# 62 instead of 26 of the 128 half operations on gathered rows in the scoring stage, on one Trainium2 core

## The chip, the cores and the metric

The kernel runs on one core of one Trainium2 chip. The metric is the device time of one execution in microseconds, the median of several runs. The engines are TensorE (PE; PEld is its weight load), VectorE (DVE), ScalarE (ACT), GpSimd (POOL) and SyncE (SP), which here only issues loads.

## What is computed

One residual block on 256 tokens of width 2048: a mixing layer (attention and a gated part), then a PEER retrieval layer with 16384 experts, then a final norm. The change is in the retrieval layer:

```python
def one_block(xb):
    q = (xb @ w_q).reshape(T, PEER_HEADS, 2, PEER_HALF)
    sc = jnp.einsum('thcd,hckd->thck', q, sub_keys)
    ...
    idx = e1 * PEER_N_KEYS + e2
    g = jax.nn.softmax(best.astype(jnp.float32), axis=-1)
    u_sel = jnp.take(u_tab, idx, axis=0)
    act = jax.nn.gelu(jnp.einsum('td,thkd->thk', xb, u_sel))
    v_sel = jnp.take(v_tab, idx, axis=0)
    return jnp.einsum('thk,thkd->td', g.astype(act.dtype) * act, v_sel)
```

Each token picks 8 x 16 = 128 experts. A row of `peer_u` per pick gives a score, and the rows of `peer_v`, weighted by gate times gelu of the score, are summed.

## The kernel before

Two groups of tokens are treated in two ways. For ND = 224 tokens nothing is gathered: the kernel multiplies with all 16384 rows of both tables and lets the gates be zero where a row was not picked. For the other NS = 32 tokens the picked rows are gathered: 32 tokens x 4 slots fill the 128 partitions, and NG = 32 rounds bring one row of `peer_u` and later one of `peer_v` to each partition. Every row comes in two halves of 1024 numbers, so there are 4 x NG = 128 half operations: numbers 0 to 63 on `peer_u` (a product with the token and a sum, L1079), and 64 to 127 on `peer_v` (scaled and added to an accumulator, L1082 and L1085). `half_rows(k)` on VectorE does number k; `gather(k)` on GpSimd (L386) brings its 0.52 MB (128 rows of 4 KB) into one of the two halves of the tile PICKED, as soon as half operation k-2 has read it.

**Scoring stage** (about 470 to 1244 us). 128 steps j, each with two units of `u_t`, 0.52 MB each, through a ring of six slots. SP loads a unit (L321) when the slot's former unit is used up; ACT rounds it to its high part (HI, `top`, L588); VectorE subtracts for the low part (RING_LO, `low`, L1032); TensorE does eight high matmuls (L1428) and, one unit later, eight low ones (L1434). When both units of step j are through, ACT copies the low half of the result (`low_half_out`, L622, tile HOLES), VectorE adds it (`sum_halves`, L1042), ACT applies gelu. Behind the sum stand, at steps from 2 on, pieces of the choice of experts, and, at the steps named in HALF_STEPS, one half operation.

From step SPREAD0 = 60 to 115 the gates of the 224 tokens are also spread over the 16384 experts, four tokens a step: VectorE multiplies the product of the step before into the store (`apply_gates`, L1060) and makes second one-hots (L1050); ACT puts the rest of that product (`put_gates`, L647, which waits for L1060) and makes first one-hots (L632, L635); TensorE multiplies the two (`spread`, L1398, into a PSUM bank); VectorE also gates the newest scores (`land`, L1068). Each engine runs its queue in the order of the code. In ACT's loop a step is:

```python
            for j in range(NKEYS):
                top(2 * j + 4)
                if j:
                    gelu(j - 1)
                if 0 <= j - 1 - SPREAD0 < N_BATCH:
                    put_gates(j - 1 - SPREAD0)
                if 0 <= j - SPREAD0 < N_BATCH:
                    first_one_hots(j - SPREAD0)
                top(2 * j + 5)
                low_half_out(j)
```

and in VectorE's: the two `low` of step j+1, `apply_gates`, `second_one_hots`, `land`, `sum_halves(j)`, the half operation.

**Value stage** (about 1244 to 1957 us). 256 units v of `peer_v` (a half of the columns for each of the 128 steps, then the other half) go through the same ring and the same `top` and `low`. Here the stored products are the moving operand: ACT rounds them (`weight_hi`, L681, tile WHL), VectorE makes their remainder (`weight_lo`, L1116), TensorE does eight high matmuls (L1468) and, one unit later, eight low ones (L1473). In ACT's queue `weight_hi(v+3)` stands behind `top(v+4)`, so TensorE's unit v+3 waits for the load of unit v+4. The half operations that are not in the scoring stage stand at the units in HALF_UNITS, spread evenly. Between the two halves of columns VectorE empties eight banks (L1122).

GpSimd's queue holds, in order: some `low` (until step 60), the first gathers, the two loads of X1R behind the end of the scoring stage, the other gathers, with the load of FG among them.

Of the kernel before, what the change touches and what calls it, by code (L numbers as in the profile page):

```python
# [26 lines left out]
PH, TOPK, NKEYS = 8, 16, 128  # L27
# [43 lines left out]
SPREAD0 = 60  # L71
SPREAD_END = SPREAD0 + N_BATCH
# [16 lines left out]


HALVES = 4 * NG
HALF_STEPS = list(range(SPREAD0 + 2, SPREAD_END, 4)) + list(range(SPREAD_END, NKEYS))
HALF_UNITS = [1 + i * 248 // (HALVES - len(HALF_STEPS)) for i in range(HALVES - len(HALF_STEPS))]
LAST_DOT = HALF_UNITS[2 * NG - 1 - len(HALF_STEPS)]
S_BANKS = 3
# [21 lines left out]
def hybrid_peer_block(nc, x, w_in, w_out, wq_t, keys_t, u_t, peer_u, peer_v, ws_t, bs_t, gain_t, ffn_gain, z_gain,  # L117
                      out_gain, subln_gain, final_gain, lambdas, rope, out):
    ctx = ExitStack()
    with ctx:  # L120
# [210 lines left out]
        def _(pool):  # L331
# [48 lines left out]
            def gather(k):  # L380

                table = peer_u if k < 2 * NG else peer_v
                g, half = k % (2 * NG) // 2, k % 2
                if k >= 2:
                    pool.wait_ge(halves, k - 1)
                pool.indirect_dma_start(PICKED[:, half * HALF:(half + 1) * HALF], None,  # L386
                                        table.rearrange("e (a c) -> (e a) c", a=2),
                                        bass.IndirectOffsetOnAxis(PK4[:, half, g:g + 1], 0)).then_inc(row_ready[half], 16)
# [14 lines left out]
            pool.wait_ge(x4_scaled, 1)  # L403
            for k in range(len(HALF_STEPS) + 2):
                gather(k)
            pool.wait_ge(low_used, N_U)
            for tt in range(TT):
                pool.dma_start(X1R[:, tt, :], x1_dram[tt * P:(tt + 1) * P, :]).then_inc(x1_back, 16)
            for k in range(len(HALF_STEPS) + 2, HALVES):
                u = HALF_UNITS[k - 2 - len(HALF_STEPS)]  # L410
                if u >= NKEYS + 32 and HALF_UNITS[k - 3 - len(HALF_STEPS)] < NKEYS + 32:
                    pool.wait_ge(low_used, N_U + NKEYS + 24)
# [1142 lines left out]
```

## Time and profile before

| | |
|---|---|
| median of 3 runs | 1994.64 us (1987.77 to 2002.11) |
| profiled execution | 1981.4 us, span of its core 1979.6 us |
| PE / PEld busy | 93% / 85% |
| DVE, ACT, POOL busy | 69%, 53%, 18% |
| read from HBM | 421.29 MB, 215 GB/s over the span |
| gathers | 64 from peer_u, 64 from peer_v |

The profile shows one execution. Busy times count instructions at work; an idle time is put down to what ended it, as the semaphores tell. A matmul's time overlaps that of the next. PEclk is the clock that TensorE was granted, as a share of 2.4 GHz.

### The profile page before, as it was taken

How to read it: one execution, taken by the hardware profiler on the slowest of the kernel's cores; microseconds unless marked ns; L12 is line 12 of the kernel's file. 1: busy time of each engine (PE TensorE's matmuls, PEld its weight loads, DVE VectorE, ACT ScalarE, POOL GpSimd, SP SyncE). 2: the span in 40 equal slices, each digit the busy share in tenths (PEclk: the TensorE clock that was granted, in tenths of full speed). 3: DMA queues.
4: the chain of work that ended last, by engine and by line, in shares of the span. 5: the costliest groups of instructions: out<-in, count | busy, mean ns of one | idle time of the engine just before them, and what ended most of it. 6: DMA issues, size and time to landing. Idle time of an engine off the chain costs nothing. (4 is left out here: it accounts for less than half of the span.)

```text
span 1979.6 us, 29432 instructions
## 1 busy us (share of the span) xinstructions
PE 1846.3 (93%) x10926; PEld 1675.0 (85%) x10926; DVE 1368.1 (69%) x2269; ACT 1042.2 (53%) x1815; POOL 362.3 (18%) x213
## 2 busy tenths in 40 slices
PE   7999989899999999988898889899999999999996
PEld 6887777789989999888888889888988988888886
DVE  4446775654798888666666677776766777677676
ACT  5454644434555555766666664454444444444444
POOL 1003330100420530000000003222222222222220
PEclk9999999999999999999999999999999999999999
DMA  7665435765667676555555558887888878878883
GB/s 247 185 186 155 148 117 177 245 192 179 193 200 209 205 221 208 186 174 173 170 166 175 171 173 297 296 265 264 282 261 265 273 249 272 274 261 274 271 264 116
DMA packets 116197, 427.62 MB, mean 216 GB/s; under 512 B 13088, under 2 KB 13184, under 8 KB 115008
## 3 DMA queue, kind: packets, MB, share of 16 engines
q1 hardware_dynamic: 95472, 347.65, 55.7%
q0 software_dynamic: 20448, 77.67, 11.6%
q8 instruction: 84, 1.38, 0.3%
q10 hardware_dynamic: 144, 0.52, 0.1%
q14 instruction: 49, 0.40, 0.1%
HBM read 421.29 MB, written 4.51 MB: 215 GB/s over the span
## 5 line engine op out<-in xcount | busy, mean ns | idle before, releaser
L588 ACT ACTIVATE HI<-RING_RAW 128x1024 fp32r<-128x1024 f32 x512 | 541.9, 1058 | 544.6 <-DMA RING_RAW<-peer_v 372.3
L1032 DVE TENSOR_TENSOR RING_LO<-RING_RAW,HI 128x1024 fp32r<-128x1024 f32 x481 | 586.7, 1237 | 1.8
L1468 PE MATMUL PS<-WHL,HI 128*128 128x448 f32 x2048 | 472.8, 374 | 50.0 <-DVE WHL L1116 48.4
L1428 PE MATMUL PS<-xT,HI 128*128 128x448 f32 x2048 | 465.7, 369 | 0.0
L1468 PEld LDWEIGHTS PS<-WHL,HI 128*128 128x128 f32 x2048 | 371.2, 191 | 86.1 <-ACT HI L588 38.1
L1428 PEld LDWEIGHTS PS<-xT,HI 128*128 128x128 f32 x2048 | 366.4, 189 | 24.6
L1434 PEld LDWEIGHTS PS<-xT,RING_LO 128*128 128x128 f32 x2048 | 265.9, 191 | 16.2 <-DVE RING_LO L1032 4.4
L1473 PEld LDWEIGHTS PS<-WHL,RING_LO 128*128 128x128 f32 x2048 | 270.2, 192 | 7.2
L1434 PE MATMUL PS<-xT,RING_LO 128*128 128x224 f32 x2048 | 269.5, 274 | 2.6 <-DVE RING_LO L1032 1.8
L1473 PE MATMUL PS<-WHL,RING_LO 128*128 128x224 f32 x2048 | 271.0, 275 | 0.0
L735 DVE TENSOR_TENSOR LO<-RAW,HI 128x1024 fp32r<-128x1024 f32 x124 | 155.8, 1259 | 139.2 <-PE PS L1221 103.1
L421 ACT ACTIVATE HI<-RAW 128x1024 fp32r<-128x1024 f32 x144 | 153.1, 1065 | 168.1 <-PE PS L1221 56.4
L1116 DVE TENSOR_TENSOR WHL<-store,WHL 128x224 fp32r<-128x224 f32 x256 | 99.8, 390 | 204.2 <-ACT WHL L681 202.8
L386 POOL DMA_INDIRECT PICKED<-peer_u,PK x64 | 106.5, 1664 | 656.3 <-DVE DOTS L1079 655.9
L386 POOL DMA_INDIRECT PICKED<-peer_v,PK x64 | 110.0, 1720 | 324.2 <-DVE ACC L1085 305.9
L1216 PE MATMUL PS<-HI,xT 128*128 128x512 f32 x444 | 141.9, 401 | 1.7 <-ACT HI L421 1.0
L1221 PE MATMUL PS<-HI,xT 128*128 128x512 f32 x444 | 138.6, 394 | 0.0
L1042 DVE TENSOR_TENSOR TMP<-PS,HOLES 128x224 f32<-128x224 f32 x68 | 26.6, 392 | 140.7 <-ACT HOLES L622 139.9
L377 POOL TENSOR_TENSOR RING_LO<-RING_RAW,HI 128x1024 fp32r<-128x1024 f32 x31 | 74.6, 2407 | 251.5 <-DVE store L1042 251.5
L1398 PE MATMUL PS<-HOLES,ONE 128*128 128x128 f32 x448 | 64.6, 287 | 38.8 <-ACT ONE L635 38.8
L1221 PEld LDWEIGHTS PS<-HI,xT 128*128 128x128 f32 x444 | 84.2, 190 | 18.2
L1216 PEld LDWEIGHTS PS<-HI,xT 128*128 128x128 f32 x444 | 81.2, 190 | 17.9 <-DVE xT L762 1.1
(204 smaller groups left out, 1683.6 us busy)
## 6 DMA issues: line engine op xcount, KB each, us to landing
RING_RAW<-u_t SPq DMA_DIRECT2D x256, 512.0 KB, 4.4
RING_RAW<-peer_v SPq DMA_DIRECT2D x256, 512.0 KB, 5.7
RAW<-w_in SPq DMA_DIRECT2D x80, 512.0 KB, 3.6
RAW<-w_out SPq DMA_DIRECT2D x32, 512.0 KB, 4.4
RAW<-wq_t SPq DMA_DIRECT2D x32, 512.0 KB, 4.4
x_spill<-X POOLq DMA_DIRECT2D x2, 1024.0 KB, 6.0
X1R<-x_spill POOLq DMA_DIRECT2D x2, 1024.0 KB, 7.2
out<-X1R SPq DMA_DIRECT2D x4, 512.0 KB, 3.7
```

The lines of the kernel that those rows point to most:

```text
L386: pool.indirect_dma_start(PICKED[:, half * HALF:(half + 1) * HALF], None, table.rearrange("e (a c) -> (e a) c", a=2), bass.IndirectOffsetO ...
L421: nc.scalar.activation(HI[:, slot, :], RAW[:, slot, :], ACT.Copy).then_inc(hi_ready, 1)
L588: nc.scalar.activation(HI[:, n % HI_SLOTS, :], RING_RAW[:, n % RING, :], ACT.Copy).then_inc(top_ready, 1)
L735: v.tensor_tensor(LO[:, u % 2, :], RAW[:, u % 4, :], HI[:, u % 4, :].bitcast(FP32), ALU.subtract).then_inc(lo_ready[u % 2], 1)
L1032: v.tensor_tensor(RING_LO[:, n % RING, :], RING_RAW[:, n % RING, :], HI[:, n % HI_SLOTS, :].bitcast(FP32), ALU.subtract).then_inc(low_dve, 1)
L1116: v.tensor_tensor(WHL[:, u % W_SLOTS, 1, :], store[:, u % NKEYS, :], WHL[:, u % W_SLOTS, 0, :].bitcast(FP32), ALU.subtract).then_inc(w_lo, 1)
L1216: mm(banks[c], high(tt), h[:, halves[c]], start=first, stop=False)
L1221: ins = mm(banks[c], low(tt), h[:, halves[c]], start=False, stop=last and tt > 0)
L1428: return mm(PS[:, j % S_BANKS, 0:2 * ND].rearrange("p (a t) -> p a t", a=2), HI[:, n % HI_SLOTS, kk * P:(kk + 1) * P], xT[:, k, :, 0:ND], ...
L1434: return mm(PS[:, j % S_BANKS, 0:ND], RING_LO[:, n % RING, kk * P:(kk + 1) * P], xT[:, k, 0, 0:ND], start=False, stop=k == KT - 1)
L1468: return mm(PS[:, V_BANKS[i], 0:2 * ND].rearrange("p (a t) -> p a t", a=2), HI[:, v % HI_SLOTS, i * P:(i + 1) * P], WHL[:, v % W_SLOTS, :, :],
L1473: return mm(PS[:, V_BANKS[i], 0:ND], RING_LO[:, (N_U + v) % RING, i * P:(i + 1) * P], WHL[:, v % W_SLOTS, 0, :], start=False, stop=v % NKE ...
```

## The change

```diff
 HALVES = 4 * NG
-HALF_STEPS = list(range(SPREAD0 + 2, SPREAD_END, 4)) + list(range(SPREAD_END, NKEYS))
+HALF_STEPS = list(range(SPREAD0 + 6, NKEYS))
 HALF_UNITS = [1 + i * 248 // (HALVES - len(HALF_STEPS)) for i in range(HALVES - len(HALF_STEPS))]
```

SPREAD0 is 60, SPREAD_END 116, NKEYS 128. HALF_STEPS was 62, 66, ... 114 (14 steps) and 116 to 127 (12); it is now 66 to 127 (62). HALF_UNITS follows: 102 units 2 or 3 apart before, 66 units 3 or 4 apart now. Everything else that depends on the number (the split of GpSimd's queue, the unit at which the dots are finished: 90 before, 4 now) is computed from it.

VectorE's queue at the first of the changed steps, step 62: L1042 is the sum of step 62, L1079 the half operation with its read of the sum (two rows), L1032 the subtractions for step 63.

```order
 L1068 TENSOR_TENSOR store<-store,TMP 128x8
 L1042 TENSOR_TENSOR TMP<-PS,HOLES 128x224
-L1079 ISA PICKED,DOTS<-PICKED,X_96 128x1024
-L1079 ISA DOTS 128x1
 L1032 TENSOR_TENSOR RING_LO<-RING_RAW,HI 128x1024 x2
 L1060 TENSOR_TENSOR store<-store,PS 128x62x4
```

The half operation of step 62 is gone. The same queue at step 67 and the start of step 68:

```order
 L1068 TENSOR_TENSOR store<-store,TMP 128x28
 L1042 TENSOR_TENSOR TMP<-PS,HOLES 128x224
+L1079 ISA PICKED,DOTS<-PICKED,X_96 128x1024
+L1079 ISA DOTS 128x1
 L1032 TENSOR_TENSOR RING_LO<-RING_RAW,HI 128x1024 x2
 L1060 TENSOR_TENSOR store<-store,PS 128x67x4
```

Between the sum and the subtractions for the next step there is now a half operation, and so it is at every step to 115 that had none.

GpSimd's queue from the return of the picks (PK) on; x_spill is where X1R is loaded from:

```order
 L400 DMA PK_107<-spk_spill 32x3x32 x4
 L377 TENSOR_TENSOR RING_LO<-RING_RAW,HI 128x1024 x9
-L386 DMA PICKED<-peer_u,PK_107 128x1024 x28
+L386 DMA PICKED<-peer_u,PK_107 128x1024 x64
 L408 DMA X1R<-x_spill 128x2048 x2
-L386 DMA PICKED<-peer_u,PK_107 128x1024 x36
-L386 DMA PICKED<-peer_v,PK_107 128x1024 x30
+L386 DMA PICKED<-peer_v,PK_107 128x1024 x43
 L413 DMA FG<-final_gain 128x2048
```

The loads of X1R stand behind all 64 gathers of peer_u now, and only gathers of peer_v are left behind them.

## Rows read from the trace of the kernel before

**Rows 1.** Busy us by stage: window, length, PE, PEld, DVE, ACT, POOL, PEclk, DMA share, GB/s.

```profile
800.00:1181.00 381.00, 342.19 (x2219) 318.53 (x2218) 252.56 (x524) 259.46 (x607) 23.48 (x14) 1.00 0.56 174
1181.00:1244.00 63.00, 56.71 (x360) 53.28 (x358) 51.02 (x77) 32.60 (x53) 18.82 (x12) 0.99 0.83 283
1244.00:1952.00 708.00, 663.70 (x4055) 620.85 (x4056) 503.75 (x659) 336.44 (x507) 173.21 (x104) 0.99 0.80 266
```

**Rows 2.** Timeline, a step without half operation: start us, us, engine, line, operation [idle before].

```profile
1110.62 0.34 ACT L622 ACTIVATE HOLES<-PS 128x224 f32<-128x224 f32 x1
...
1111.04 0.39 DVE L1042 TENSOR_TENSOR TMP<-PS,HOLES 128x224 f32<-128x224 f32 x1 [2.21 <-ACT HOLES L622]
1111.35 2.35 DVE L1032 TENSOR_TENSOR RING_LO<-RING_RAW,HI 128x1024 fp32r<-128x1024 f32 x2
...
1113.62 0.58 DVE L1060 TENSOR_TENSOR store<-store,PS 128x420 f32<-128x420 f32 x1
...
1116.31 1.04 ACT L588 ACTIVATE HI<-RING_RAW 128x1024 fp32r<-128x1024 f32 x1
1116.46 1.16 PE L1398 MATMUL PS<-HOLES,ONE 128*128 128x128 f32 x8 [0.45 <-ACT ONE L635]
1117.26 0.34 ACT L622 ACTIVATE HOLES<-PS 128x224 f32<-128x224 f32 x1
```

**Rows 3.** Timeline of the value stage around one late load.

```profile
1634.28 7.87 SPq L321 DMA_DIRECT2D RING_RAW<-peer_v  x4
...
1636.60 1.79 PE L1468 MATMUL PS<-WHL,HI 128*128 128x448 f32 x8
...
1639.11 1.79 PE L1468 MATMUL PS<-WHL,HI 128*128 128x448 f32 x8
...
1641.61 1.06 ACT L588 ACTIVATE HI<-RING_RAW 128x1024 fp32r<-128x1024 f32 x1 [3.51 <-DMA RING_RAW<-peer_v]
...
1642.98 0.39 DVE L1116 TENSOR_TENSOR WHL<-store,WHL 128x224 fp32r<-128x224 f32 x1 [3.32 <-ACT WHL L681]
...
1643.52 1.66 PE L1468 MATMUL PS<-WHL,HI 128*128 128x448 f32 x7 [1.73 <-DVE WHL L1116]
```

**Rows 4.** Line L1468: count, min/median/max ns, first and last start us.

```profile
L1468 PE MATMUL PS<-WHL,HI x2048: 358/365/742, 1244.1 to 1956.1; 128*128 128x448 f32 x187
```

**Rows 5.** Loads by median us to landing, in 500 to 700, 1250 to 1934, 1935 to 1955.

```profile
RING_RAW<-u_t SPq DMA_DIRECT2D x76, 512.0 KB, 4.5
...
RING_RAW<-peer_v SPq DMA_DIRECT2D x246, 512.0 KB, 5.7
...
RING_RAW<-peer_v SPq DMA_DIRECT2D x4, 512.0 KB, 4.9
```

**Rows 6.** Timeline, a step with a half operation.

```profile
1173.17 0.39 DVE L1042 TENSOR_TENSOR TMP<-PS,HOLES 128x224 f32<-128x224 f32 x1 [2.14 <-ACT HOLES L622]
1173.48 1.22 DVE L1079 CUSTOM_DVE_ANT_0 PICKED<-PICKED,X 128x1024 f32<-128x1024 f32 x1
...
1179.74 1.16 PE L1398 MATMUL PS<-HOLES,ONE 128*128 128x128 f32 x8 [1.59 <-ACT ONE L635]
...
1180.96 0.39 DVE L1042 TENSOR_TENSOR TMP<-PS,HOLES 128x224 f32<-128x224 f32 x1 [2.12 <-ACT HOLES L622]
```

**Rows 7.** The sum of step 60; then groups of 800 to 1181: busy, mean ns, idle before.

```profile
800.11 0.39 DVE L1042 TENSOR_TENSOR TMP<-PS,HOLES 128x224 f32<-128x224 f32 x1 [2.22 <-ACT HOLES L622]
...
L1398 PE MATMUL PS<-HOLES,ONE 128*128 128x128 f32 x448 | 64.6, 287 | 38.8 <-ACT ONE L635 38.8
...
L1079 DVE CUSTOM_DVE_ANT_0 PICKED<-PICKED,X 128x1024 f32<-128x1024 f32 x14 | 17.0, 1216 | 0.0
```

**Rows 8.** Timeline: TensorE's first matmuls of the value stage.

```profile
1244.12 6.15 PE L1468 MATMUL PS<-WHL,HI 128*128 128x448 f32 x16 [5.82 <-DVE WHL L1116]
```

**Rows 9.** GpSimd's timeline: two of the gathers that begin late behind the former.

```profile
1259.95 1.71 POOL L386 DMA_INDIRECT PICKED<-peer_u,PK  x1 [7.52 <-DVE DOTS L1079]
...
1884.09 1.68 POOL L386 DMA_INDIRECT PICKED<-peer_v,PK  x1 [7.82 <-DVE ACC L1085]
```

## The prediction

> **What bounds the kernel now.** I read, in this order, a table of busy time by stage, the timeline of single steps, the groups of instructions with the idle time before them, and the times that loads take to land. The reader should see in the table that TensorE (PE) is the busiest engine, and where it is not full: 342.2 of 381.0 us while the gates are spread (800 to 1181), 663.7 of 708 in the value stage [rows 1]. These two stretches have different limits, and the change takes work from the second and puts it into the first.
>
> In the spreading stretch the timeline of one step without a half operation shows a ring that goes through two engines [rows 2]. From one low-half copy on ScalarE (ACT, L622) to the next the starts are: sum on VectorE (DVE, L1042) 0.42 us later, its two subtractions (L1032) 0.31 later, the gating product (L1060) 2.27 later; then on ACT, behind that product, the put (L647), the first one-hots (L632, L635) and the next rounding (L588), which starts 2.69 later, and the next copy 0.95 after it. That is 6.64 us, the whole step, with no slack: each item waits for the one before it, or stands behind it in its queue. TensorE is not in the ring. It waits 0.45 us in each such step for the one-hots, before its eight spreading products (L1398). VectorE is idle too, 2.2 us in each step, but ahead of the sum, where it waits for the copy.
>
> In the value stage TensorE sets the pace when nothing is late: a unit (eight high and eight low matmuls) starts 2.51 us after the one before, 1636.60 to 1639.11 [rows 3]. All 2048 high matmuls start between 1244.1 and 1956.1, 712.0 us [rows 4]; 255 units at 2.51 and the last unit's 1.4 make 641.5. So 70.5 us are lost. The releasers of the idle time are DVE's WHL and ACT's HI, and both stand behind a DMA. The rows of one loss show it: a load of peer_v issued at 1634.28 lands, and ACT rounds it at 1641.61, 7.33 us later; only behind this rounding, in ACT's queue, comes the weight (L681) of the unit before, then DVE's remainder of it (L1116) at 1642.98, and TensorE starts at 1643.52 instead of 1641.62, 1.90 us late [rows 3]. So a load has 7.33 less 1.90, about 5.4 us, to land. The median load of this stage takes 5.7, in the last 20 us, where no gather is left, 4.9, and the u_t loads of a stretch without gathers took 4.5 [rows 5]. The gathers are what pushes loads over the limit.
>
> **What moves.** From the code: before, 14 half operations stand at steps 62, 66 to 114 and 12 at steps 116 to 127; now one stands at each step 66 to 127, which keeps the last 12 and has 50 in place of 14 in the spreading stretch, 36 more. The value stage has 66 instead of 102. Nothing is added in all, and each gather on GpSimd's queue moves with its half operation, two ahead.
>
> **The scoring stage.** The moved operation (L1079) stands right behind the sum, inside the ring: sum at 1173.17, half operation at 1173.48 [rows 6], and the subtractions only behind that. The step from sum to sum is 1180.96 less 1173.17, 7.79 us, against 6.64 without one [rows 2, 6]. TensorE waits 1.59 instead of 0.45. The long row agrees: from the sum of step 60 (800.11) to that of step 115 (1180.96) are 55 steps, 380.85 us [rows 6, 7]; 55 at 6.64 are 365.2, and 15.7 us for the 14 half operations [rows 7] are 1.12 each. I take 1.14, from the added wait of TensorE. VectorE's 2.2 us of idle time do not cover it: that wait ends with ACT's copy, which moves too. 36 times 1.14 is **+41.0 us**. The bounds are narrow, 39 to 43: the 36th, at step 115, leads into a step that lacks the one-hots and may be half hidden, and longer waits could come from the gathers. The latter I cost at nothing: a gather is issued two half operations ahead, 15.5 us now, and lands in under 10; the DMA moved 174 GB/s in this stretch [rows 1], and 3 transfers of 0.52 MB in 7.8 us are 202 GB/s, which the stretch without gathers also moved (76 loads of 0.52 MB in 200 us) [rows 5].
>
> Steps 116 to 127 keep 12 half operations in both kernels, and TensorE was busy 56.7 of 63 us there, 5.8 of the rest being one wait at the changeover [rows 1, 8]: 0, give or take 2. On GpSimd's queue the two X1R loads now stand behind 64 gathers instead of 28, but the last of them is released at step 127 in both; 0. The change of the dots into gates comes at units 4 and 8 instead of 90 and beyond, with the same instructions; 0 to 1.
>
> **The value stage.** It loses 36 half operations and 36 gathers. VectorE is busy 503.8 of 708 us there [rows 1] and not the bound, so its 36 times 1.3 us are worth nothing by themselves; what is regained is the late loads. Of the 70.5 us lost about 2 are the first units at half clock [rows 8] and about 4 the flush between the two halves of columns; 64.5 remain for the 101 gathers issued in this stage, 0.64 us each. Their neighbours stand 2 or 3 units apart. If the price is per gather, 36 fewer give back 36 times 0.64, **-23.0 us**. Both ends are open, since the trace has no gather that stands alone: a gather may cost as much as the one loss shown, 1.9 us for the two gathers in flight, that is 0.95 each, so that 65 of them cost 62 and only 3 us come back; or half of today's price when its neighbour is far off, 21 in all, so that 44 come back. I take 0.64, as it is the mean of all of them: by the timeline the 14 gathers that stand more than 9 us behind the one before (first and last in [rows 9]) were followed by 0.68 us of loss each, the other 84 by 0.66.
>
> **Sum.** 41.0 less 23.0 is +18.0 us. The profiled execution took 1981.4 us for its span of 1979.6, so 1999.4. It is faster than all three timed runs, whose median is 1994.6, 13.2 above; the sum goes onto the median: 2012.6, and I say 2012, +0.9%.
>
> **Rivals.** (a) *The losses stay.* The loads go on being late, one stall for each gather that stands alone, where now two gathers 4 us apart share one. At 0.95 each the stage gives back 3 us and the kernel is +38 us, 2033. It decides from 0.66 us a gather on: there 64.5 less 65 times 0.66 is 21, the net 20, and the kernel over 1% slower. For it speaks the shown stall, and that 5.4 us is only 0.5 above the unloaded 4.9; against it that many gathers pass without any stall. The Trainium skill has a rule that would lead to the same end, on the page "DMA: Bandwidth & Descriptors", section "Latency and other measured facts": reads from HBM whose rows lie a large power of two apart ran at 207 GB/s for a 512 KiB pitch and 164 for 2 MiB. A load of peer_v has a pitch of 1 MiB, and by that rule the loads alone would need 2.5 to 3.2 us a unit, gathers or not; the time would come out near +41. The trace does not bear it out: the stage moves 266 GB/s, gathers included [rows 1], and units follow at 2.51 us wherever no load is late.
> (b) *Gathers that stand alone cost half.* Then 44 us come back, the net is -3, 1992, no change. For it speaks that a lone gather overlaps fewer loads; against it the 14 above.
> (c) *The half operation hides in VectorE's idle time*, or nearly no losses are left in the value stage. Either makes the net about -20: 1975, faster. Against the first stand the 14 steps of 7.8 us [rows 6]; for the second there is nothing but the distance.
> (d) *TensorE's clock falls.* It will wait 1.6 us in every one of 50 steps in a row instead of in every fourth. The granted clock was 0.5, that is 1.2 GHz, at the start of the value stage behind a wait of 5.82 us, and 16 high matmuls took 6.15 us there [rows 8], where eight take 1.79 [rows 3]. A step at this level is 6.15 for its 16 high matmuls, half of that for the 16 low ones with half the columns, and 1.2 for the spreading: 10.4, or 2.6 over the new step. In half of the 50 steps that is 65 us more, 2077. Against it: the 14 steps with 1.6 us of waiting had clock 1.00 throughout [rows 1]. The Trainium skill speaks against the change here ("TensorE: Matmul & The Clock Gate", section "A second HAM failure mode: psum-queue depth-cycling"): many short idle times between groups of matmuls made the clock swing. The row of today has none of it at one long wait in four; steps in a row are not shown.
>
> **How the numbers follow.** Forecast 0.64, with an own range of 2000 to 2024; (a) 0.16; (b) 0.12; (c) 0.04; (d) 0.04. A measurement of this kernel tells about 1%, 20 us, from no change. The forecast lies just inside; with its width some 0.24 of its 0.64 falls beyond. So slower 0.24 + 0.16 + 0.04 = 0.44, within 1% 0.40 + 0.12 = 0.52, faster 0.04. The range, 1991 to 2035, takes in (a) and (b) at their own values.
>
> **What would show it.** In the changed profile: sums (L1042) of steps 66 to 115 all 7.8 us apart, the idle time of L1398 from 38.8 us [rows 7] to near 38.8 + 36 times 1.14, 80 us; ACT and DVE rows in the same order as in [rows 6]; the value stage beginning 41 us later, near 1285, and lasting 689 us instead of 712. If the first holds and the value stage lasts over 700, (a) was right; under 675, (b) or (c). Clock 0.5 in rows of the spreading stretch would be (d). Steps of 6.7 us with half operations would overthrow the ring itself.

## The result, and the profile after

| | before | changed |
|---|---|---|
| runs | 1987.77, 2002.11, 1994.64, 1997.3 | 2014.72, 2027.51, 2024.31, 2033.8 |
| median us | 1995.97 | 2025.91 |
| profiled execution | 1981.4, span 1979.6 | 2014.7, span 2012.9 |

The ratio is 1.0148 with an interval of 1.0087 to 1.021: slower by 1.5%, 30 us. In the pair of profiled executions it is 33.3 us; the profiled one of the kernel before, 1981.4, is faster than all four of its timed runs, which matters below for what a single profile can tell. The forecast was +18.

The stages of the changed kernel, in the columns of [rows 1]; its scoring stage ends at 1282, not 1244. The rows are the spreading stretch and the value stage:

```profile
800.00:1222.00 422.00, 343.45 (x2222) 319.68 (x2221) 294.16 (x597) 258.58 (x606) 83.30 (x50) 1.00 0.60 200
...
1282.00:1988.00 706.00, 665.66 (x4077) 622.47 (x4077) 462.64 (x587) 337.35 (x508) 111.65 (x68) 0.99 0.75 240
```

In the value stage VectorE does 41 us less, GpSimd 62 us less, and the DMA moves 240 GB/s instead of 266. The stage is hardly shorter for it in this pair.

The spreading steps, first the sums of steps 60 and 115, then one step with its half operation, to be laid beside [rows 6]:

```profile
798.51 0.39 DVE L1042 TENSOR_TENSOR TMP<-PS,HOLES 128x224 f32<-128x224 f32 x1 [2.21 <-ACT HOLES L622]
...
1101.01 1.16 PE L1398 MATMUL PS<-HOLES,ONE 128*128 128x128 f32 x8 [1.58 <-ACT ONE L635]
...
1102.23 0.39 DVE L1042 TENSOR_TENSOR TMP<-PS,HOLES 128x224 f32<-128x224 f32 x1 [2.23 <-ACT HOLES L622]
1102.54 1.22 DVE L1079 CUSTOM_DVE_ANT_0 PICKED<-PICKED,X 128x1024 f32<-128x1024 f32 x1
...
1218.97 0.39 DVE L1042 TENSOR_TENSOR TMP<-PS,HOLES 128x224 f32<-128x224 f32 x1 [2.12 <-ACT HOLES L622]
```

From step 60 to 115 it is 420.5 us, 39.6 more than the 380.9 of [rows 6, 7]. The 35 added half operations in these 55 intervals come to 1.13 each; TensorE waits 1.58 us before the spreading product of this step, as in the others. The group of those products shows the same in one row (800 to 1222), 78.6 us of idle time where [rows 7] has 38.8:

```profile
L1398 PE MATMUL PS<-HOLES,ONE 128*128 128x128 f32 x442 | 63.9, 287 | 78.6 <-ACT ONE L635 78.5
```

The value stage, by the first and last start of its high matmuls as in [rows 4], and TensorE's waits for a weight (us in all, times, the longest):

```profile
L1468 PE MATMUL PS<-WHL,HI x2048: 358/365/743, 1281.7 to 1988.5; 128*128 128x448 f32 x187
```

```profile
PE PS L1468 <- DVE WHL L1116: 45.2, 44, 6.4
```

It begins 37.6 us later than before, and lasts 706.8 us instead of 712.0. So 5.2 us came back between these two profiles, where 23 were forecast. 37.6 less 5.2 is 32.4 of the 33.3 us; the rest lies behind the stage.

A loss of the changed kernel, to be laid beside [rows 3]. Here one gather is in flight alone, issued at 1652.70 behind 7.32 us of waiting:

```profile
1652.70 1.68 POOL L386 DMA_INDIRECT PICKED<-peer_v,PK  x1 [7.32 <-DVE ACC L1085]
...
1659.10 1.79 PE L1468 MATMUL PS<-WHL,HI 128*128 128x448 f32 x8
...
1661.36 1.06 ACT L588 ACTIVATE HI<-RING_RAW 128x1024 fp32r<-128x1024 f32 x1 [3.04 <-DMA RING_RAW<-peer_v]
1662.32 0.37 ACT L681 ACTIVATE WHL<-store 128x224 fp32r<-128x224 f32 x1
...
1663.27 1.04 PE L1468 MATMUL PS<-WHL,HI 128*128 128x448 f32 x4 [1.49 <-DVE WHL L1116]
```

ScalarE's weight (L681) needs no load at all: it copies from the store. It starts at 1662.32 only because the rounding ahead of it in the queue waited 3.04 us for its load. TensorE starts 1.66 us late (1659.10 + 2.51 is 1661.61). With one gather in flight the loss is here nearly the 1.90 us of [rows 3], where two, issued at 1632.61 and 1637.16, were in flight.

### The profile page after: what moved, and what is told of

Same layout as the page of the kernel before. It is cut to its first block, busy times and chain, and to the rows that moved or that the text cites. A ratio compares the mean times of both kernels' runs of the same rounds, so it can differ in the third digit from the quotient of the medians.

```text
span 2012.9 us, 29432 instructions
## 1 busy us (share of the span) xinstructions
PE 1845.3 (92%) x10926; PEld 1674.3 (83%) x10926; DVE 1365.3 (68%) x2269; ACT 1040.5 (52%) x1815; POOL 360.3 (18%) x213
## 4 chain that ended last, share of the span: by engine, by line
PE 50%; DVE 17%; DMA 15%; ACT 10%; issue 6%; POOL 1%; ACTq 0%; DVEq 0%; POOLq 0%; SPq 0%
DMA RING_RAW<-peer_v 13%; PE PS L1468 12%; PE PS L1428 8%; DVE RING_LO L1032 7%; PE PS L1473 6%; PE PS L1434 5%; PE PS L1216 4%; PE PS L1221 4%; ACT ONE L632 3%; ACT HI L588 3%; DVE PICKED L1079 3%; PE PS L1238 3%; PE PS L1225 2%; PE PS L1219 2%; PE PS L1248 1%
## 5 line engine op out<-in xcount | busy, mean ns | idle before, releaser
L1032 DVE TENSOR_TENSOR RING_LO<-RING_RAW,HI 128x1024 fp32r<-128x1024 f32 x481 | 586.9, 1237 | 1.8
L1468 PE MATMUL PS<-WHL,HI 128*128 128x448 f32 x2048 | 471.9, 373 | 46.7 <-DVE WHL L1116 45.2
L1468 PEld LDWEIGHTS PS<-WHL,HI 128*128 128x128 f32 x2048 | 369.4, 190 | 82.9 <-ACT HI L588 36.3
L1398 PE MATMUL PS<-HOLES,ONE 128*128 128x128 f32 x448 | 64.6, 287 | 78.6 <-ACT ONE L635 78.5
L1398 PEld LDWEIGHTS PS<-HOLES,ONE 128*128 128x128 f32 x448 | 54.2, 191 | 88.2 <-ACT ONE L635 88.2
L1042 DVE TENSOR_TENSOR TMP<-PS,HOLES 128x224 f32<-128x224 f32 x68 | 26.7, 392 | 137.4 <-ACT HOLES L622 136.6
L647 ACT ACTIVATE store<-PS 128x272 f32<-128x272 f32 (+55 forms) x56 | 17.1, 306 | 163.0 <-DVE store L1060 163.0
```

What stands on the lines that cost most here:

```text
L1032: v.tensor_tensor(RING_LO[:, n % RING, :], RING_RAW[:, n % RING, :], HI[:, n % HI_SLOTS, :].bitcast(FP32), ALU.subtract).then_inc(low_dve, 1)
L1398: last = mm(PS[:, G_BANK + b % 2, t * NKEYS:(t + 1) * NKEYS].rearrange("p (q c) -> p q c", q=4), ONE1[:, t, :], ONE2[:, 4 * t:4 * t + 4, : ...
L1468: return mm(PS[:, V_BANKS[i], 0:2 * ND].rearrange("p (a t) -> p a t", a=2), HI[:, v % HI_SLOTS, i * P:(i + 1) * P], WHL[:, v % W_SLOTS, :, :],
```

## The experiments

Twelve more runs were made, in three groups; each group has its own runs of the kernel before (medians 1987.7 and 1994.2, and one run of 1988.6). Where one run is named, a difference in the total of under 20 us says little by itself; the argument rests on the length of the value stage in the trace. Expectations count the value stage from its first to its last unit start (705.3 us in the changed kernel); the rows give the last matmul's start, 1.5 us later (706.8). "Loss" below is the length by the rows less the 641.5 us of the prediction.

The three theories of the first group were: 1, gathers make loads late, and each one alone has its price; 2, the loads of peer_v are slow by themselves; 3, VectorE's half operations hold up the weights.

**no_value_gathers**

```diff
-                gather(k)
+                if k < 2 * NG:
+                    gather(k)
...
-                dve.wait_ge(row_ready[half], 16 * (k // 2 + 1))
+                dve.wait_ge(row_ready[half], 16 * (min(k // 2 + 1, NG)))
```

> The changed kernel without the 64 gathers of peer_v; its half operations on VectorE stay and read what PICKED holds, so the expert values of 32 tokens are left out. Theory 1 (each gather that stands alone delays one load and costs 0.9 us): the 255 unit starts of the value stage take 640 to 650 us instead of 705.3, and the whole is near 1955. Theory 2 (the loads of peer_v are late by themselves, for the pitch of their rows): it stays at 700 or more. Theory 3 (the half operations on VectorE are what delays the weights): it stays near 700 too.

Measured: 1968.2 us in one run. The code has one line more here, so the high matmuls are line L1469.

```profile
L1469 PE MATMUL PS<-WHL,HI x2048: 358/365/742, 1284.6 to 1941.8; 128*128 128x448 f32 x187
```

The stage takes 657.2 us (655.7 in the expectation's count), the loss is 15.7, a little over the expected span. All half operations were there, and the same peer_v loads: neither makes more than these 15.7 us without gathers. Theory 1 stands; 2 falls, and 3 as a cause by itself. The prediction had set aside only 6 us for what is not the gathers'.

**lone_value_gathers**

```diff
-                gather(k)
+                if k < 2 * NG or k % 2 == 0:
+                    gather(k)
...
-                dve.wait_ge(row_ready[half], 16 * (k // 2 + 1))
+                dve.wait_ge(row_ready[half], 16 * (min(k // 2 + 1, NG) if half else k // 2 + 1))
```

> The changed kernel with every second gather of peer_v left out, so that the 32 others stand 7 to 8 units apart; all half operations stay, the odd ones read old data (values of 32 tokens left out in part). Theory 1: 32 gathers at 0.9 us and about 6 us at the ends, 640 + 35 = 675 us for the value stage. A price that halves again with the distance: 655. Theory 2 or 3: 700 or more.

Measured: 1999.9 us in one run.

```profile
L1469 PE MATMUL PS<-WHL,HI x2048: 358/365/742, 1281.2 to 1974.6; 128*128 128x448 f32 x187
```

693.4 us, a loss of 51.9, 17 us over what 0.9 a gather gives and far over the halved price. 32 gathers make 36.2 us of loss over the run without any, 1.13 each. A gather far from the next costs more than the mean of the 65 in the changed kernel, which is 0.76 by the same sum (65.3 less 15.7).

**sixteen_value_gathers** has the same edit with `k % 4 == 0` and the waits for it.

> The changed kernel with 16 of the 64 gathers of peer_v, 15 units apart (values of 32 tokens left out in part, half operations kept). If a gather that stands quite alone costs 1.1 us, as the step from 0 to 32 gathers showed, the loss is 16 + 18 = 34 us and the stage 674; if the price of 0.64 held for every gather, 26 and 666.

Measured: 1986.4 us in one run.

```profile
L1469 PE MATMUL PS<-WHL,HI x2048: 358/365/742, 1284.2 to 1959.3; 128*128 128x448 f32 x187
```

675.1 us by this row, 673.6 in the expectation's count: a hit. 16 gathers make 17.9 us, 1.12 each.

**changed_again** is the changed kernel once more.

> The changed kernel once more, on the chip of the other runs, for the spread of its value stage: by theory 1 and by every other theory steps of 7.78 us and the same time as before plus 1.5%, 2015 to 2020 where before is 1988; if the value stage here is 10 us or more off 705.3, differences below that between single profiles say nothing.

Measured: median 2024.7 of two runs, ratio to before 1.0154 (1.0128 to 1.018).

```profile
L1468 PE MATMUL PS<-WHL,HI x2048: 358/365/714, 1285.7 to 1999.4; 128*128 128x448 f32 x187
```

713.7 us, 6.9 more than in the first profile. So the 5.2 us that came back between the first two profiles are inside the spread of this stage. With this run the series is complete; the waits are the row "PE PS <- DVE WHL" of each run, the number of times that TensorE waited for a weight:

| gathers in the stage | loss us | waits |
|---|---|---|
| 0 | 15.7 | 4 |
| 16 | 33.6 | 17 |
| 32 | 51.9 | 30 |
| 64 or 65 (changed; again) | 65.3; 72.2 | 44; 39 |
| 101 (before) | 70.5 | 51 |

The first 32 gathers add 26 waits and 1.1 us each. The next 32 add 13 to 20 us together. The 36 that the change takes out, with 36 half operations beside them, make no difference that these profiles tell from zero. The last line is likely low: its profile is of an execution of 1981.4 us, and the 21 timed runs of the kernel before have a median of 1989.8. If those 8 us lie in this stage, which was not seen, its loss is near 79. The rows of the first, second and last line of the table:

```profile
PE PS L1469 <- DVE WHL L1117: 10.8, 4, 6.5
```

```profile
PE PS L1469 <- DVE WHL L1117: 23.1, 17, 6.3
```

```profile
PE PS L1468 <- DVE WHL L1116: 48.4, 51, 5.8
```

**value_halves_8_wide**, and again in the third group

```diff
-                    ins = v.scalar_tensor_tensor(ACC4[:, cols], PICKED[:, cols], DOTS[:, 0, g:g + 1], ACC4[:, cols],
+                    one = slice(half * HALF, half * HALF + 8)
+                    ins = v.scalar_tensor_tensor(ACC4[:, one], PICKED[:, one], DOTS[:, 0, g:g + 1], ACC4[:, one],
```

> The changed kernel with all gathers, but the 62 half operations of L1085 treat 8 columns instead of 1024 (the accumulation of the other columns is left out). Theory 1: the value stage stays within 5 us of 705. Theory 3: it falls by 30 us or more.

> The run with 8-column half operations once more. If VectorE's operation takes part in the loss, the value stage is again 15 to 25 us below the 705 to 712 of the changed kernel; if the 688 of the first run was spread, it comes back above 700.

Measured: 1997.8 and 2003.9 us; stages of 689.6 and 693.0. Neither expectation of the first run holds: the stage is 14 to 24 us below the two profiles of the changed kernel, and the repeat shows that this is no spread. VectorE's operation takes part in the loss as long as there are gathers. Without them, where it was kept, it has at most a share in the 15.7 us; and it shows only in this order of the queues, since the run weight_first, below, keeps both the operations and the gathers and loses 7.5 us.

**value_half_before_weight**

```diff
                 low(N_U + u + 2)
+                if u in HALF_UNITS:
...
                 if u + 2 < N_V:
                     weight_lo(u + 2)
-                if u in HALF_UNITS:
...
```

> The changed kernel with the half operation of the value stage between VectorE's low(u+2) and weight_lo(u+2), where it waits for ScalarE's weight, instead of behind both. If the operation takes part in the loss by standing in front of the next unit's work, the stage falls by 10 to 20 us from 705 to 712; if only the loads matter, it stays; if it now stands in the weight's way, it rises.

Measured: 2019.3 us, a stage of 708.2 (1285.1 to 1993.3). No change. So the operation does not act by standing behind the weight's remainder instead of ahead of it. Nor does VectorE wait for a gather to land: no wait of the value stage in the changed kernel's trace is put down to one. By what it acts stays open: a shorter one also issues the next gather some 1.2 us earlier, and this was not tried by itself.

**weight_first** turns two orders in the value stage:

```diff
-                if N_U + v + 4 < N_U + N_V:
-                    top(N_U + v + 4)
                 if v + 3 < N_V:
                     weight_hi(v + 3)
+                if N_U + v + 4 < N_U + N_V:
+                    top(N_U + v + 4)
...
-                low(N_U + u + 2)
                 if u + 2 < N_V:
                     weight_lo(u + 2)
+                low(N_U + u + 2)
```

> The changed kernel with two orders turned in the value stage: on ScalarE weight_hi(v+3) ahead of top(v+4), on VectorE weight_lo(u+2) ahead of low(u+2), so that a load may land some 2.5 to 3 us later before TensorE waits. All gathers stay. Theory 1 (late loads behind gathers, read through the in-order queue): the loss of the value stage falls from 65 us to under 20, the stage to 650 to 660, the time to 1965. If the gathers hurt by bandwidth as such, or by VectorE's work, it stays near 700.

Measured: median 1958.5 of two runs, ratio 0.9822 (0.9799 to 0.9846).

```profile
1283.00:1932.00 649.00, 647.36 (x4079) 614.70 (x4079) 462.35 (x589) 336.25 (x507) 116.00 (x68) 0.99 0.80 261
```

```profile
L1468 PE MATMUL PS<-WHL,HI x2048: 358/365/712, 1283.2 to 1932.2; 128*128 128x448 f32 x187
```

649.0 us, a loss of 7.5, with every gather in place. TensorE is busy 647.4 of 649 us, and the DMA moves 261 GB/s, more than the 240 of the changed kernel: so bandwidth was not what held it up before. What the gathers cost, they cost through the order of the queues.

**weight_first_scalar_only** has the first half of that edit.

> The changed kernel with only ScalarE's order turned (weight_hi ahead of top), VectorE's as it was. VectorE still makes low(n) ahead of weight_lo(n), so a load may land about 1.5 us later than in the changed kernel, not 3. Theory 1: most of the loss goes, 15 to 30 us of it stay; the value stage takes 655 to 670 us. If VectorE's order was what mattered, it stays above 690.

Measured: 1964.2 us in one run, a stage of 653.4 (1284.3 to 1937.7), a loss of 11.9, less than expected. ScalarE's order is the one that matters; the profile with VectorE's turned as well is 4.4 us shorter, which two single profiles hardly tell from nothing.

**weight_first_of_before** has both edits in the kernel before.

> The kernel before with the same two orders turned: 102 half operations and 101 gathers in the value stage. Theory 1: the stage falls to 650 to 665 us and the time to about 1930, and the changed kernel with these orders is slower than this one by 35 to 41 us, since nothing is left for the change to give back. If the density of gathers sets a floor of its own, the stage stays above 680.

Measured: median 1923.0 of two runs, ratio 0.9644 (0.9621 to 0.9667).

```profile
L1468 PE MATMUL PS<-WHL,HI x2048: 362/365/739, 1243.4 to 1896.7; 128*128 128x448 f32 x187
```

653.3 us with 101 gathers, and the changed kernel with the same edits is 35.5 us slower in the medians, as expected. In the two profiles its value stage starts 39.8 us later (1283.2 against 1243.4) and is 4.3 us shorter.

This also tells better what came back between the kernels as they were. Ten profiles are of the changed kernel or of kernels that differ from it only in the value stage; they enter that stage between 1281.2 and 1285.7 us, 1283.7 in the mean. The two of the kernel before do so at 1244.1 and 1243.4. The scoring stage thus costs 39.9 us. The medians differ by 30 us, and by 30.5 in the repeat, whose interval is 25.5 to 36. So some 10 us came back, 4 to 14 by that interval: more than the 5.2 of the first pair, and less than half of the 23.

**half_before_sum**

```diff
+            pool.wait_ge(summed, NKEYS)
...
+                if j in HALF_STEPS:
+                    half_rows(HALF_STEPS.index(j))
                 sum_halves(j)
                 for _ in range(PIECE_COUNT.get(j, 0)):
                     piece()
-                if j in HALF_STEPS:
-                    half_rows(HALF_STEPS.index(j))
```

> The changed kernel with the half operation ahead of the sum in VectorE's step, where VectorE waits 2.2 us for ScalarE's copy. If the ring through the copy and the sum makes the cost, steps 66 to 115 fall from 7.78 to 6.63 us and the time by 50 times 1.15, 57 us: near 1957 in a profile, ratio to before 0.985. If the cost came from the gather's traffic or from VectorE's total work, they stay at 7.7.

The added wait of GpSimd keeps the loads of X1R behind the last sum, which the last half operation now precedes.

Measured: median 1969.9 of six runs, ratio to before 0.9914 (0.9877 to 0.995). One step of its trace, from copy to copy (lines are one higher):

```profile
1099.01 0.34 ACT L623 ACTIVATE HOLES<-PS 128x224 f32<-128x224 f32 x1
1099.43 0.39 DVE L1043 TENSOR_TENSOR TMP<-PS,HOLES 128x224 f32<-128x224 f32 x1 [1.05 <-issue]
...
1103.80 1.21 DVE L1080 CUSTOM_DVE_ANT_0 PICKED<-PICKED,X 128x1024 f32<-128x1024 f32 x1
...
1104.85 1.16 PE L1399 MATMUL PS<-HOLES,ONE 128*128 128x128 f32 x8 [0.45 <-ACT ONE L636]
...
1105.65 0.34 ACT L623 ACTIVATE HOLES<-PS 128x224 f32<-128x224 f32 x1
```

The step is 6.64 us again, with a half operation in it, and TensorE's wait is back at 0.45. The value stage starts at 1229.5 instead of 1281.7, 52.2 us earlier. The same 1.22 us of VectorE cost 1.14 a step behind the sum and nothing in front of it. The ratio of 0.9914 is short of the expected 0.985. Of the 14 us by which its profile (1971.1) misses 1957, 5 are missing in the scoring stage (52.2 instead of 57) and 9.5 are the value stage, which took 716.3 us here, the longest of all.

**both_mended** joins the last edit and that of weight_first.

> The changed kernel with the half operation ahead of the sum and the value stage's orders turned. If the two costs are separate they add: 50 to 57 us from the spreading steps and 45 to 50 from the value stage, 1910 to 1915 in a profile, ratio to before near 0.963.

Measured: median 1904.7 of four runs, ratio to before 0.9549 (0.9524 to 0.9574). The stage starts at 1228.4 and takes 650.7 us: both gains are there, and the time is 5 to 10 us below the expected span. This version beats both kernels, and also the kernel before with the turned orders (0.9644).

## Why the prediction was right and where it was wrong

The sign, and that the measured 2025.9 lies in the range of 1991 to 2035, were right. The forecast's size was not: +30 instead of +18, just outside the forecast's own range of 2000 to 2024 and nearer to rival (a), 2033, than to the 2012 said. The range holds it because it was made wide enough for (a), and the chances leaned the other way, with 0.52 on a change of under 1%. The scoring term was right by its mechanism; the value term was mis-sized.

- *The scoring stage, +41.0.* Right, by its own steps: 7.78 us a step from 66 to 115, 1.13 us for each half operation, TensorE's idle time 78.6 us against the 80 said, clock 1.00 throughout. The 36th, at step 115, was not hidden. That the place in the ring makes the price, and not the work, is shown by half_before_sum. The start of the value stage moved by 37.6 in the first pair, where 1.6 us were gone before step 60 and 1.6 between step 116 and the stage, and by 39.9 in the mean of the profiles.
- *Steps 116 to 127, the X1R loads and the dots, 0.* Right within 2 us.
- *The value stage, -23.0.* This step failed. It reads "I take 0.64, as it is the mean of all of them", and takes away 36 gathers at the mean price of 101. What came back was 5.2 us in the first pair of profiles and some 10 by the medians, 0.14 to 0.28 for each gather taken out. The loss does not grow in proportion: gathers that stand alone cost 1.1 us each, the mean of the 65 that are left is 0.76 to 0.87, and the last 36 of 101 cost the least. The mean was also too high to begin with: only 6 us were set aside for the rest, where the run without gathers loses 15.7, which leaves 0.54 for each of the 101 and not 0.64. The upper end of the price, 0.95, was read from a single loss with two gathers in flight, and was itself too low for gathers alone. What the prediction named against (a), that the 14 gathers more than 9 us behind their forerunner were followed by no larger losses, was no evidence: eleven of them had a follower 4.0 to 4.8 us behind, while a gather took 7.4 us (median) to land, so they were not alone.
- *Rival (a)* had the right course: "one stall for each gather that stands alone, where now two gathers 4 us apart share one". Its price of 0.95, with 3 us given back, was not met exactly. The numbers of waits in the table fit it, 13 more waits for the first 16 gathers, and 7 to 12 more for the last 36. How a shared stall comes about (a wait of TensorE also puts off the deadlines of the loads that are already in flight) was argued, not shown.
- *The mechanism of the late load*, the rounding that waits for its load in front of the weight, was right: turning the order takes 58 us and more of loss away in both kernels (706.8 and 713.7 to 649.0, and 712.0 to 653.3). The prediction had it, but went on to price gathers and did not ask what the order itself costs.
- *Rival (b)*, half price for gathers alone, fell by the runs with 16 and 32. *Rival (c)* fell: nothing of the half operation is hidden behind the sum, though all of it is in front of it, and the value stage kept its losses. *Rival (d)* fell: the clock stayed at 1.00 over 50 steps in a row with 1.58 us of waiting each (800 to 1222). The rule of the Trainium skill on large pitches, on the page "DMA: Bandwidth & Descriptors", section "Latency and other measured facts", is not what makes the loss: its figures are for copies of 16 KiB rows between tensors in HBM. Here the same loads of 4 KB rows let the stage run in 657.2 us without gathers and, with the orders turned, in 649.0 us with them.

## What to carry to other kernels

A loss that is shared by events close together must not be priced by its mean: when events are thinned out, each that is left can cost more. The slope is shown by runs with fewer of them, down to none. Where an engine works off its queue in order, look at what stands behind an instruction that waits for a DMA; an item that needs no load should stand in front of it. And an idle time of an engine inside a ring of waits covers added work that stands in front of the instruction that waits, and not work behind it.

## What the runs showed of the hardware

Half operations of 1024 and of 8 columns differ by 14 to 24 us over the value stage while gathers run, though VectorE is busy only 65% there (462.6 of 706 us), and though the whole loss without gathers, the same operations included, is 15.7 us. The cause was not found. And the length of the stage is spread by some 10 us between executions (706.8, 713.7 and, in half_before_sum, 716.3, with one and the same program from there on), while with ScalarE's order turned four profiles lie within 649.0 and 653.4. The spread is there only where late loads reach TensorE; that they make it is likely, and not shown.
